# A transformer layer with a grouped mixture of experts on one core: the steps between the first norm and the first expert are rewritten

## The chip, the core and the metric

One Trainium2 chip (trn2); the program runs on one of its cores. The metric is device microseconds (us) of one execution. A core has five engines with queues of their own: PE (TensorE; its weight loads are shown as PEld), DVE (VectorE), ACT (ScalarE), POOL (GpSimd) and SP (SyncE, which here issues nearly all DMA). Each engine takes its instructions in program order and waits for the others by semaphores.

## What is computed

256 tokens (two blocks of 128) of width 2048 go through one layer: a projection, sparse attention and an mLSTM, gates, an output projection, a layer norm, then routed experts and a gated product ("PLE"), and a second layer norm. The part around the change:

```
h = layer_norm(DN_ALPHA * h + mix @ w_out, ln1_g, ln1_b)
grp_prob = softmax(h @ w_grp + b_grp)                      # 4 groups, the best one is taken
exp_logits = (h @ w_exp + b_exp)                           # 4 experts in each group
in_grp = the 4 logits of the chosen group; e_prob = softmax(in_grp)
e_p, e_idx = top_k(e_prob, 2); e_p = e_p / sum(e_p)        # two experts of the group
h = silu(h @ w_gate[e]) * (h @ w_up[e]) * combine; ff = h @ w_down[e]
ple = (p @ w_ple) * sigmoid(h @ w_ple_gate)
out = layer_norm(DN_ALPHA * h + ff + ple, ln2_g, ln2_b)
```

## The kernel before

**Stages.** Up to 916 us the kernel is a row of dense products. Each weight tile is split into a high and a low half by ACT (L1233) and DVE (L1720), and PE multiplies three times (L574, L575, L579). The last tile gives `RES`, the rows before the first norm. From 946.9 us on PE works through the experts in pairs of experts: `up(n)` has eight slots of 16 matmul records (L1017, gate and up weights), `down(n)` has four (L1069), and between them stand the chunks of the PLE gate (L928) and the scatters back to the rows.

**The ring.** Expert and gate weights come through a ring of 8 slots of 1 MB (`moe_ring`). SP issues 207 loads, always in the same order (L445). Loads 0 to 7 go out before 918 us. Load m from the eighth on waits until `ring_used` has reached m-7, that is, until PE is done with the slot that it overwrites. PE raises `ring_used` by 2 behind each slot of `up` and `down`.

**Between norm and experts** (916 to 947 us) the order on each queue is written out by hand:

- PE: `ple_product(0..3)` (L859), the turns of the normed rows to columns `row_turn(0..7)` (L875, four transposes each, banks 4, 5, 0, 1 in turn), `router()` (L885, 16 products of the router's weights with the turned columns, bank 4), `router_turn()` (L892), `ple_product(4..6)`, `expert_counts()` (L909 to L913, five products that count how many tokens each expert has), `ple_product(7)`, a quarter of the early gate product (L928, first of its four column parts), `row_table(4)` (L965), then `first_pairs(0)` and `first_pairs(1)` (L981, the gather of the tokens of the first group: the product of `selg` with the rows' high and low halves), then `up(0)`. The other three parts of the early gate product stand behind slot 6 of `up(0)`.
- DVE: the norm (L2149), the odd column turns (L2134), then the routing: `router_logits`, `best` once per token block (L2180 the eight largest, L2181 a copy, L2182 their replacement), `group_one_hot`, `expert_logits`, `best` twice again, `experts_one_hot` (L2206, raises `r_took`), `distances`, `slots` (L2239 to L2242), `select(0)` (L2252, eight comparisons that make `selg`), `h1_low(0..3)` (L2160, the low halves of the rows by quarters), `combine`, `overflow`. Most of these are tied by `link`, which makes DVE wait for its own last result.
- ACT: `pp_copy(0..3)` (L1502, PSUM to SBUF behind each PLE product), the even column turns (L1516), `high(0)` (L1507, the high half of block 0's rows, 128x2048), `pp_copy(4)`, `pp_copy(5)`, `high(1)` (block 1), `pp_copy(6)`, `pp_copy(7)`, then two exponentials (L1620, L1622, which want another function table, ACT_TABLE_LOAD), `row_table` (L1548), and `gained(0..7)` (L1568, which turns a gathered pair into `xg`, the input of `up(0)`).

`first_pairs` is held by these waits; a pair with i of 2 or more waits until ACT has emptied the bank of pair i-2, and slot 0 of `up(0)` wants `g_act` at 2:

```
if q == 0:
    pe.wait_ge(pp_c, 8)
pe.wait_ge(h1_lo, q + 1)
for i in (2 * q, 2 * q + 1):
    if i >= 2:
        pe.wait_ge(g_act, i - 1)
    gather_pair(i, B[6 + i % 2]).then_inc(g_mm, 1)
```

Of the kernel before, what the change touches and what calls it, by code (L numbers as in the profile page):

```python
# [137 lines left out]
def build(nc, x, p, w_in, kv_norm, w_ukv, m_i_bias, m_f_bias, w_proj_a, w_proj_m, w_out, ln1_g, ln1_b,  # L138
          w_grp, b_grp, w_exp, b_exp, w_gate, w_up, w_down, w_ple, w_ple_gate, ln2_g, ln2_b, out):
    with ExitStack() as ctx:  # L140
# [120 lines left out]
        tk8, r1, r2, r3, r4 = tiny(8), tiny(32), tiny(32), tiny(32), tiny(16)  # L261
        mg, me, gd, ed = tiny(16), tiny(16), tiny(8), tiny(8)
        oneh, combw, gp, top2 = tiny(8), tiny(8), tiny(4), tiny(8)
        took, cum, tot, tslot = tiny(2 * NE), tiny(2 * NE), tiny(NE), tiny(2 * NE)
# [233 lines left out]
        def _(pl):  # L498
# [58 lines left out]
            g.iota(iota[:], pattern=[[1, CAP]], base=0, channel_multiplier=0,  # L557
# [7 lines left out]
        def _(pe):  # L565
# [312 lines left out]
            def router():  # L878

                pe.wait_ge(r_in, 32)  # L880
                pe.wait_ge(hT_act, 4)
                pe.wait_ge(hT_dve, 4)
                for k in range(KT):
                    j = 32 * (k % 4)
                    last = mm(B[4][j:j + 32, 0:TOK], wr[:, k, :], hT[:, k, :], start=k < 4, stop=k >= KT - 4)  # L885
                last.then_inc(r_part, 1)
# [11 lines left out]
            for i in range(8):  # L898
                row_turn(i)
            router()  # L900
            router_turn()
            for n in range(4, 7):
                ple_product(n)

            def expert_counts():
# [5 lines left out]
                mm(c[:, NE:2 * NE], upper[:], two, start=False, stop=True)  # L911
                mm(c[:, 2 * NE:3 * NE], ones[:], one, start=True, stop=False)
                mm(c[:, 2 * NE:3 * NE], ones[:], two, start=False, stop=True).then_inc(r_cum, 1)  # L913
# [107 lines left out]
            def up(n):  # L1021
# [7 lines left out]
                for i in range(UP_SLOTS):  # L1029
# [9 lines left out]
                    if n == 0 and i == 6:  # L1039
                        ple_rows(EW[:, 0, :], 2, 0, True, True, (1, 2, 3)).then_inc(early_used, 1)  # L1040
# [75 lines left out]
            ple_product(7)  # L1116
            pe.wait_ge(bank_free[1], 20)
            pe.wait_ge(early_in[0], 16)
            ple_rows(EW[:, 0, :], 2, 0, True, True, (0,))
            pe.wait_ge(sel_ready, 1)  # L1120
            row_table(4, selT_mm)
            pe.wait_ge(h1_hi, NT)
# [94 lines left out]
        def _(ac):  # L1217
# [286 lines left out]
            def high(a):  # L1504

                ac.wait_ge(z_ready, NT)
                fn(h1h[:, a, :, :].rearrange("p t q -> p q t"), RES[:, a, :].rearrange("p (q t) -> p q t", t=KT),  # L1507
                   ACT.Copy).then_inc(h1_hi, 1)
# [11 lines left out]
            pp_copy(4)  # L1520
            pp_copy(5)
            high(1)
            pp_copy(6)
            pp_copy(7)
            def used(kind, n, i):

                ac.wait_ge(ring_used, LOAD_AT[kind, n, i, 1] + 1)
# [178 lines left out]
        def _(dv):  # L1706
# [448 lines left out]
            def h1_low(q):  # L2155

                dv.wait_ge(h1_hi, NT)
# [358 lines left out]
```

## Time and profile before

| | |
|---|---|
| median of 3 runs | 1491.25 us (1491.24 to 1491.49) |
| the profiled execution | 1491.56 us |
| its span, first to last instruction | 1489.8 us |
| PE busy | 1462.4 us (98% of the span) |
| DVE, ACT, POOL busy | 706.8, 513.1, 57.3 us |
| DMA, over the whole span | 405.92 MB, mean 272 GB/s |
| granted TensorE clock, mean | 0.998 |

Times in the profile are us from the first instruction. A row of the timeline gives start, duration, engine, line, operation, what it writes and reads, and the form; consecutive instructions of one line on one engine are merged (x8), and the bracket tells how long the engine sat idle before it and what ended that.
### The profile page before, as it was taken

To read this page: it belongs to the slowest core of one execution; us is meant where nothing else is said; L and a number is where in the kernel's file an instruction comes from. 1 tells how busy PE (TensorE), PEld (TensorE's weight loads), DVE (VectorE), ACT (ScalarE), POOL (GpSimd) and SP (SyncE) were. 2 spreads that over 40 slices of the span, in tenths; PEclk is the share of its full clock that TensorE was granted. 3 is DMA by queue.
4 is the path that set the end of the run, shared out by engine and by line. 5 is a ranking of instruction groups with operands and counts; after the bars stand their busy time and mean duration, and the time that the engine had idled before them with its cause. 6 is when DMAs were issued, how large, how long until landed. Compare 5 with 4: busy or idle time off the path is not lost.

```text
span 1489.8 us, 16743 instructions
## 1 busy us (share of the span) xinstructions
PE 1462.4 (98%) x6572; PEld 997.4 (67%) x6572; DVE 706.8 (47%) x974; ACT 513.1 (34%) x690; POOL 57.3 (4%) x63
## 2 busy tenths in 40 slices
PE   9999999999999999999999999999999998999998
PEld 7887788888778888888888887534434443454443
DVE  5546675467656665454555555431221231143336
ACT  4444444455545454444444434411000100031111
POOL 0000000053300000000000000000000000000000
PEclk9999999999999999999999999999999999999999
DMA  8654586754454585655567977599999999999995
GB/s 311 201 169 162 167 238 197 226 197 142 142 195 142 184 241 193 199 187 190 190 209 229 349 238 244 209 419 421 416 411 419 394 388 420 417 393 415 415 407 212
DMA packets 138287, 405.92 MB, mean 272 GB/s; under 512 B 14296, under 2 KB 18016, under 8 KB 113248
## 3 DMA queue, kind: packets, MB, share of 16 engines
q1 hardware_dynamic: 129472, 396.52, 73.0%
q10 hardware_dynamic: 8736, 8.33, 1.7%
q8 instruction: 51, 0.84, 0.2%
q14 instruction: 28, 0.23, 0.0%
HBM read 392.76 MB, written 4.20 MB: 266 GB/s over the span
## 4 chain that ended last, share of the span: by engine, by line
PE 92%; DMA 5%; DVE 1%; ACT 0%; issue 0%; POOL 0%; SPq 0%; POOLq 0%; DVEq 0%; ACTq 0%
PE bank L574 19%; PE bank L575 19%; PE bank L579 19%; PE bank L1017 12%; PE bank L1069 5%; PE bank L928 5%; DMA moe_ring<-in_w_gate_dram 3%; DMA moe_ring<-in_w_down_dram 2%; PE bank L981 2%; PE bank L1112 1%; PE bank L1097 1%; PE bank L1113 1%; PE bank L733 1%; PE bank L755 1%; PE bank L950 1%; PE bank L951 1%
## 5 line engine op out<-in xcount | busy, mean ns | idle before, releaser
L1720 DVE TENSOR_TENSOR w_lo<-w_ring,w_hi 128x1024 fp32r<-128x1024 f32 (+1 forms) x312 | 381.4, 1225 | 286.1 <-ACT w_hi L1233 285.0
L1233 ACT ACTIVATE w_hi<-w_ring 128x1024 fp32r<-128x1024 f32 (+1 forms) x312 | 327.3, 1051 | 329.8 <-PE bank L579 329.8
L574 PE MATMUL bank<-w_hi,xT_hi 128*128 128x512 f32 (+1 forms) x864 | 344.3, 399 | 1.7 <-ACT w_hi L1233 1.7
L575 PE MATMUL bank<-w_hi,xT_lo 128*128 128x512 f32 (+1 forms) x864 | 334.6, 387 | 0.0
L1017 PE MATMUL bank<-moe_ring,xg 128*64 128x512 f32 x1024 | 226.1, 594 | 10.4 <-DMA moe_ring<-in_w_gate_dram 6.7
L579 PE MATMUL bank<-w_lo,xT_hi 128*128 128x512 f32 (+1 forms) x864 | 229.1, 387 | 0.0
L574 PEld LDWEIGHTS bank<-w_hi,xT_hi 128*128 128x128 f32 x864 | 162.3, 188 | 38.5 <-issue 4.6
L575 PEld LDWEIGHTS bank<-w_hi,xT_lo 128*128 128x128 f32 x864 | 162.4, 188 | 32.8 <-issue 1.9
L579 PEld LDWEIGHTS bank<-w_lo,xT_hi 128*128 128x128 f32 x864 | 161.5, 188 | 32.9
L1017 PEld LDWEIGHTS bank<-moe_ring,xg 128*64 128x64 f32 x1024 | 72.9, 137 | 156.7 <-issue 156.1
L1069 PE MATMUL bank<-moe_ring,moe_hiddenT 128*64 128x512 f32 x448 | 100.2, 595 | 1.8 <-DMA moe_ring<-in_w_down_dram 1.8
L2323 DVE TENSOR_TENSOR res<-res,bank 128x512 f32<-128x512 f32 x62 | 38.4, 681 | 105.3 <-issue 80.4
L1069 PEld LDWEIGHTS bank<-moe_ring,moe_hiddenT 128*64 128x64 f32 x448 | 31.6, 137 | 61.7 <-issue 60.4
L928 PE MATMUL bank<-moe_ring,h1T 128*128 128x512 f32 x144 | 63.4, 593 | 0.0
L2286 DVE TENSOR_TENSOR ple_sig<-bank,ple_sig 128x512 f32<-128x512 f32 x24 | 15.5, 686 | 73.8 <-PE bank L928 57.1
L574 PE MATMUL bank<-w_hi,mixT_hi 128*128 128x512 f32 x128 | 50.1, 391 | 0.0
L575 PE MATMUL bank<-w_hi,mixT_lo 128*128 128x512 f32 x128 | 49.8, 389 | 0.0
L574 PE MATMUL bank<-w_hi,ymT_hi 128*128 128x512 f32 x128 | 49.8, 389 | 0.0
L574 PE MATMUL bank<-w_hi,yaT_hi 128*128 128x512 f32 x128 | 49.8, 389 | 0.0
L575 PE MATMUL bank<-w_hi,yaT_lo 128*128 128x512 f32 x128 | 49.8, 389 | 0.0
L575 PE MATMUL bank<-w_hi,ymT_lo 128*128 128x512 f32 x128 | 49.8, 389 | 0.0
L928 PEld LDWEIGHTS bank<-moe_ring,h1T 128*128 128x128 f32 x144 | 27.2, 190 | 31.6 <-issue 31.0
(292 smaller groups left out, 1352.0 us busy)
## 6 DMA issues: line engine op xcount, KB each, us to landing
w_ring<-in_w_in_dram SPq DMA_DIRECT2D x103, 1024.0 KB, 5.0
moe_ring<-in_w_gate_dram SPq DMA_DIRECT2D x64, 1024.0 KB, 9.7
moe_ring<-in_w_up_dram SPq DMA_DIRECT2D x64, 1024.0 KB, 10.5
moe_ring<-in_w_down_dram SPq DMA_DIRECT2D x64, 1024.0 KB, 11.1
w_ring<-in_w_proj_a_dram SPq DMA_DIRECT2D x16, 1024.0 KB, 5.1
w_ring<-in_w_proj_m_dram SPq DMA_DIRECT2D x16, 1024.0 KB, 5.1
w_ring<-in_w_out_dram SPq DMA_DIRECT2D x16, 1024.0 KB, 5.2
moe_ring<-in_w_ple_gate_dram SPq DMA_DIRECT2D x15, 1024.0 KB, 13.2
```

Of the source, the lines that this page charges most:

```text
L574: mm(b, lh(k, m), WH[:, s, kk, 0:width], start=start and kk == 0, stop=False)
L575: mm(b, ll(k, m), WH[:, s, kk, 0:width], start=False, stop=False)
L579: last = mm(b, lh(k, m), WL[:, s, kk, 0:width], start=False, stop=stop and kk == 1)
L733: last = mm(B[4 + j][:, r * w:r * w + w], aqT[:, 4 * (u % 4) + 2 * j + r, a * P:a * P + P], kT[:, 0:w], start=True, stop=True)
L928: ins = mm(B[b + a][:, :], hT[:, k, a * P:a * P + P], w[:, t * NC:t * NC + NC], start=first and t == 0, stop=last and t == 3)
L981: last = mm(b[:, kk * TOK:kk * TOK + TOK], src[:, a, 2 * i + kk, :], selg[:, a, :], start=part == 0 and a == 0, stop=part == 1 and a == 1)
L1017: last = mm(B[b0 + i % 2][CAP * e:CAP * e + CAP, :], xg[:, k, (e0 + e) * CAP:(e0 + e) * CAP + CAP], w[e][:, t * NC:t * NC + NC], start=k = ...
L1069: last = mm(B[4 + c][CAP * e:CAP * e + CAP, :], src[:, k, CAP * e:CAP * e + CAP], w[e][:, c * NC:c * NC + NC], start=k == 0, stop=k == 3)
L1233: fn(WH[:, h % 4, :, 0:width], W32[:, h // 2, 2 * (h % 2):2 * (h % 2) + 2, 0:width], ACT.Copy).then_inc(hi_ready, 1)
L1720: v.tensor_tensor(WL[:, h % 4, :, 0:width], W32[:, h // 2, 2 * (h % 2):2 * (h % 2) + 2, 0:width], WH[:, h % 4, :, 0:width].bitcast(F32), A ...
L2286: last = v.tensor_tensor(psg[:, a, :], B[b + a][:, :], psg[:, a, :], ALU.add)
L2323: v.tensor_tensor(r, r, B[b0 + a][:, :], ALU.add).then_inc(y_add, 1)
```

## The change

Five edits, all between the first norm and the end of `up(0)`:

1. The router's 16 products go out in four steps of four, step 0 after `row_turn(5)`, the rest after `row_turn(7)`; they write bank 2 in place of bank 4.
2. The routing on DVE handles both token blocks in one call of `best`; three copies go; `slots` is one instruction in place of four (the count's table starts at 1 in place of 0, and the totals are copied later, in `combine`); `expert_counts` raises `r_cum` after three of its five products.
3. `select` makes `selg` in two comparisons of 128x256 in place of eight of 128x64.
4. `high` goes by quarters of the columns for both blocks (two instructions of 128x512 each), placed between the `pp_copy` calls; the last comes after `pp_copy(7)`. `h1_low(q)` waits for quarter q alone.
5. On PE: two in place of three PLE products before `expert_counts`, `ple_product(6)` after it, then `row_table(4)`, then `ple_product(7)`. The first part of the early gate product moves behind slot 6 of `up(0)`, to the other three.

```diff
-            g.iota(iota[:], pattern=[[1, CAP]], base=0, channel_multiplier=0,
+            g.iota(iota[:], pattern=[[1, CAP]], base=1, channel_multiplier=0,
...
-            def router():
-                pe.wait_ge(r_in, 32)
-                pe.wait_ge(hT_act, 4)
-                pe.wait_ge(hT_dve, 4)
-                for k in range(KT):
+            def router(step):
+                if step == 0:
+                    pe.wait_ge(r_in, 32)
+                    pe.wait_ge(bank_free[1], 20)
+                pe.wait_ge(hT_act, step + 1)
+                pe.wait_ge(hT_dve, step + 1)
+                for k in range(4 * step, 4 * step + 4):
                     j = 32 * (k % 4)
-                    last = mm(B[4][j:j + 32, 0:TOK], wr[:, k, :], hT[:, k, :], start=k < 4, stop=k >= KT - 4)
-                last.then_inc(r_part, 1)
+                    last = mm(B[2][j:j + 32, 0:TOK], wr[:, k, :], hT[:, k, :], start=step == 0, stop=step == 3)
+                if step == 3:
+                    last.then_inc(r_part, 1)
...
-            for i in range(8):
+            for i in range(6):
                 row_turn(i)
-            router()
+            router(0)
+            row_turn(6)
+            row_turn(7)
+            for step in range(1, 4):
+                router(step)
             router_turn()
-            for n in range(4, 7):
-                ple_product(n)
+            ple_product(4)
+            ple_product(5)
...
                 mm(c[:, NE:2 * NE], ones[:], one, start=True, stop=False)
-                mm(c[:, NE:2 * NE], upper[:], two, start=False, stop=True)
-                mm(c[:, 2 * NE:3 * NE], ones[:], one, start=True, stop=False)
-                mm(c[:, 2 * NE:3 * NE], ones[:], two, start=False, stop=True).then_inc(r_cum, 1)
+                mm(c[:, NE:2 * NE], upper[:], two, start=False, stop=True).then_inc(r_cum, 1)
+                mm(B[3][:, 0:NE], ones[:], one, start=True, stop=False)
+                mm(B[3][:, 0:NE], ones[:], two, start=False, stop=True).then_inc(r_cum, 1)
...
                     if n == 0 and i == 6:
-                        ple_rows(EW[:, 0, :], 2, 0, True, True, (1, 2, 3)).then_inc(early_used, 1)
+                        pe.wait_ge(early_in[0], 16)
+                        ple_rows(EW[:, 0, :], 2, 0, True, True).then_inc(early_used, 1)
...
             expert_counts()
-            ple_product(7)
-            pe.wait_ge(bank_free[1], 20)
-            pe.wait_ge(early_in[0], 16)
-            ple_rows(EW[:, 0, :], 2, 0, True, True, (0,))
+            ple_product(6)
             pe.wait_ge(sel_ready, 1)
             row_table(4, selT_mm)
-            pe.wait_ge(h1_hi, NT)
+            ple_product(7)
             first_pairs(0)
             first_pairs(1)
...
-            def high(a):
+            def high(q):
                 ac.wait_ge(z_ready, NT)
-                fn(h1h[:, a, :, :].rearrange("p t q -> p q t"), RES[:, a, :].rearrange("p (q t) -> p q t", t=KT),
-                   ACT.Copy).then_inc(h1_hi, 1)
+                for a in range(NT):
+                    last = fn(h1h[:, a, 4 * q:4 * q + 4, :].rearrange("p t q -> p q t"),
+                              RES[:, a, :].rearrange("p (q t) -> p q t", t=KT)[:, :, 4 * q:4 * q + 4], ACT.Copy)
+                last.then_inc(h1_hi, 1)
...
             high(0)
             pp_copy(4)
+            high(1)
             pp_copy(5)
-            high(1)
+            high(2)
             pp_copy(6)
             pp_copy(7)
+            high(3)
...
-                dv.wait_ge(h1_hi, NT)
+                dv.wait_ge(h1_hi, q + 1)
...
-                v.tensor_copy(rrow[:], B[4][:, 0:TOK]).then_inc(r_row, 1)
+                v.tensor_copy(rrow[:], B[2][:, 0:TOK]).then_inc(r_row, 1)
...
+                v.tensor_tensor(two(rp)[:, :, 0:4], two(B[5][:, 0:40])[:, :, 0:4], brt[:, 0:4].unsqueeze(1).to_broadcast([P, 2, 4]),
+                                ALU.add)
                 link(v.tensor_tensor(two(lgt), two(B[5][:, 0:40]), brt.unsqueeze(1).to_broadcast([P, 2, 20]), ALU.add))
-                link(v.tensor_copy(two(rp)[:, :, 0:4], two(lgt)[:, :, 0:4]))
-            def best(a, n, found, out):
-                link(v.max(found[:, 8 * a:8 * a + 8], rp[:, 16 * a:16 * a + 16]))
-                link(v.tensor_copy(tk8[:, 0:n], found[:, 8 * a:8 * a + n]))
-                link(v.match_replace(out[:, 16 * a:16 * a + 16], tk8, rp[:, 16 * a:16 * a + 16], TAKEN))
+            def best(n, found, out):
+                for a in range(NT):
+                    last = v.max(found[:, 8 * a:8 * a + 8], rp[:, 16 * a:16 * a + 16])
+                link(last)
+                link(v.tensor_copy(two(tk8)[:, :, 0:n], two(found)[:, :, 0:n]))
+                for a in range(NT):
+                    last = v.match_replace(out[:, 16 * a:16 * a + 16], tk8[:, 8 * a:8 * a + 8], rp[:, 16 * a:16 * a + 16], TAKEN)
+                link(last)
...
-                    last = v.tensor_reduce(r4[:, 8 + 4 * a:12 + 4 * a],
+                    last = v.tensor_reduce(rp[:, 16 * a:16 * a + 4],
                                            r3[:, NE * a:NE * a + NE].rearrange("p (g e) -> p e g", g=GROUPS), AX, ALU.add)
                 link(last)
-                link(v.tensor_copy(two(rp)[:, :, 0:4], two(r4[:, 8:16])))
...
             def combine():
+                dv.wait_ge(r_cum, 2)
+                link(v.tensor_copy(tot, B[3][:, 0:NE]))
...
-                link(v.tensor_copy(cum, B[5][:, P:P + 2 * NE]))
-                link(v.tensor_copy(tot, B[5][:, P + 2 * NE:P + 3 * NE]))
-                link(v.tensor_tensor(cum, cum, took, ALU.mult))
-                link(v.tensor_scalar(tslot, cum, -1.0, None, ALU.add))
+                link(v.tensor_tensor(tslot, B[5][:, P:P + 2 * NE], took, ALU.mult))
...
                 for a in range(NT):
-                    for e in range(EPG):
-                        t = NE * a + EPG * g + e
-                        last = v.tensor_scalar(selg[:, a, CAP * e:CAP * e + CAP], iota[:], tslot[:, t:t + 1], None,
-                                               ALU.is_equal)
+                    t = NE * a + EPG * g
+                    last = v.tensor_tensor(selg[:, a, :].rearrange("p (e c) -> p e c", e=EPG),
+                                           iota[:, :].unsqueeze(1).to_broadcast([P, EPG, CAP]),
+                                           tslot[:, t:t + EPG].unsqueeze(2).to_broadcast([P, EPG, CAP]), ALU.is_equal)
```

## Rows read from the trace of the kernel before

**Rows 1.** Windows of the expert stage: us, busy times, clock, DMA share, GB/s
```profile
954.00:958.00 4.00, 4.00 (x30) 3.22 (x32) 0.00 (x0) 2.30 (x6) 0.00 (x0) 1.00 1.01 426
962.00:963.00 1.00, 1.00 (x8) 0.36 (x6) 0.00 (x0) 0.00 (x0) 0.00 (x0) 1.00 0.73 205
950.56:1447.80 497.24, 483.09 (x2154) 212.54 (x2151) 124.48 (x188) 70.81 (x116) 0.00 (x0) 1.00 1.00 409
```
**Rows 2.** Timeline of SP's queue, the ring's loads around 950 and 980 us
```profile
950.56 0.81 SPq L445 DMA_DIRECT2D moe_ring<-in_w_gate_dram  x2
...
960.57 0.80 SPq L445 DMA_DIRECT2D moe_ring<-in_w_gate_dram  x2
...
976.56 0.81 SPq L445 DMA_DIRECT2D moe_ring<-in_w_gate_dram  x2
985.49 0.80 SPq L445 DMA_DIRECT2D moe_ring<-in_w_up_dram  x2
```
**Rows 3.** Timeline, turned columns and router products
```profile
923.50 3.97 PE L875 MATMUL bank<-ident,res 128*128 128x128 f32 x32 [0.29 <-DVE res L2149]
924.78 3.72 DVE L2134 TENSOR_SCALAR h1T<-bank,small 128x256 f32<-128x256 f32 x8 [1.34 <-PE bank L875]
928.65 1.93 PE L885 MATMUL bank<-h1T,w_router 128*32 128x256 f32 x32 [1.18 <-DVE h1T L2134]
930.64 0.42 DVE L2171 COPY router_rows<-bank 128x256 f32<-128x256 f32 x1 [2.14 <-PE bank L885]
```
**Rows 4.** Timeline of DVE, the routing steps
```profile
932.29 0.18 DVE L2180 MAX8 small<-small 128x8 f32<-128x16 f32 x1
...
932.77 0.16 DVE L2182 MATCH_REPLACE8 small<-small 128x16 f32<-128x16 f32 x1
...
936.23 0.26 DVE L2206 TENSOR_TENSOR small<-small 128x16 f32<-128x16 f32 x2
```
**Rows 5.** Timeline of PE, from the counts to the first expert
```profile
936.82 0.29 PE L909 MATMUL bank<-small,upper 128*128 128x16 f32 x2
...
937.85 1.96 PE L859 MATMUL bank<-wple,pT 128*128 128x512 f32 x4
...
939.65 1.88 PE L928 MATMUL bank<-ple_early,h1T 128*128 128x512 f32 x4
...
940.97 0.96 PE L965 MATMUL bank<-ident_r,moe_sel 128*128 128x128 f32 x4
...
944.79 0.47 PE L981 MATMUL bank<-moe_sel,h_hi 128*128 128x256 f32 x2 [0.25 <-ACT xg L1568]
...
946.86 7.09 PE L1017 MATMUL bank<-moe_ring,xg 128*64 128x512 f32 x32
```
**Rows 6.** Timeline of ACT, from the last product copies to the gathered pairs
```profile
939.34 1.12 ACT L1502 ACTIVATE ple_products<-bank 128x512 f32<-128x512 f32 x2
940.47 1.28 ACT L1620 ACT_TABLE_LOAD   x1
...
941.98 0.59 ACT L1548 ACTIVATE moe_selT<-bank 128x512 fp32r<-128x512 f32 x1
...
943.63 1.97 ACT L1568 ACTIVATE xg<-bank,small 128x256 f32<-128x256 f32 x4 [1.07 <-PE bank L981]
```
**Rows 7.** Groups by form: count, busy us, mean ns of one, idle before
```profile
L1507 ACT ACTIVATE h_hi<-res 128x2048 fp32r<-128x2048 f32 x2 | 7.6, 3780 | 0.0
...
L1629 ACT ACTIVATE ln_g<-ln_g 128x2048 f32<-128x2048 f32 x1 | 1.9, 1907 | 0.0
...
L2160 DVE TENSOR_TENSOR h_lo<-res,h_hi 128x512 fp32r<-128x512 f32 x8 | 8.0, 1083 | 0.0
```
**Rows 8.** PE's first transposes, its last matmuls, and the window behind them
```profile
1.59 4.53 PE L625 MATMUL bank<-ident 128*128 128x128 f32 x20 [1.59 <-POOL ident L508]
...
1477.66 5.31 PE L1169 MATMUL bank<-res,rstd_diagonal 128*128 128x512 f32 x12
...
1482.00:1486.00 4.00, 0.98 (x3) 0.15 (x1) 0.31 (x1) 1.19 (x2) 0.00 (x0) 0.90 0.76 275
```

More of the change, by code:

```diff
@@ L260, in build @@
         brt, lgt, rp = tiny(20), tiny(40), tiny(32)
-        tk8, r1, r2, r3, r4 = tiny(8), tiny(32), tiny(32), tiny(32), tiny(16)
+        tk8, r1, r2, r3, r4 = tiny(16), tiny(32), tiny(32), tiny(32), tiny(16)
         mg, me, gd, ed = tiny(16), tiny(16), tiny(8), tiny(8)
         oneh, combw, gp, top2 = tiny(8), tiny(8), tiny(4), tiny(8)
-        took, cum, tot, tslot = tiny(2 * NE), tiny(2 * NE), tiny(NE), tiny(2 * NE)
+        took, tot, tslot = tiny(2 * NE), tiny(NE), tiny(2 * NE)
         cg, flagf, tslg = tiny(4), tiny(1), tiny(2 * EPG)
@@ L2217, in distances @@
                 for a in range(NT):
-                    last = v.tensor_scalar(ed[:, 4 * a:4 * a + 4], r4[:, 8 + 4 * a:12 + 4 * a], me[:, 8 * a:8 * a + 1], None,
+                    last = v.tensor_scalar(ed[:, 4 * a:4 * a + 4], rp[:, 16 * a:16 * a + 4], me[:, 8 * a:8 * a + 1], None,
                                            ALU.subtract)
@@ L2347, in _ @@
             router_logits()
-            best(0, 1, mg, r3)
-            best(1, 1, mg, r3)
+            best(1, mg, r3)
             group_one_hot()
             expert_logits()
-            best(0, 2, me, r1)
-            best(1, 2, me, r1)
+            best(2, me, r1)
             experts_one_hot()
```

## The prediction

> **What bounds the kernel now.** I read the windows first. From 950.56 us, when PE has used up the first ring slot, to 1447.80 the DMA engines are busy at a share of 1.00 and move 409 GB/s, while the granted clock is 1.00 and PE is busy for 483 of 497 us [rows 1]. The reader is to see that weights are delivered at the rate the engines have, from the first refill on. The queue of SP shows what starts this stream: two loads at 950.56, each pair behind one slot of `up(0)` [rows 2]. So the change can do two things alone: move the start of the stream, and make holes in it. All behind the start shifts with it; what an engine saves beside it is worth nothing.
>
> Then the timeline between norm and first expert. Two chains meet there. DVE turns columns, PE forms the router's products, DVE routes until 936.23 + 0.26 = 936.49 and then selects, and PE's `row_table` at 940.97 is the first to read the selection [rows 3 to 5]. PE fills its waits with other products. What ends last is ACT and PE in turn: the first gathered pair is emptied by ACT from 943.63, PE waits for that until 944.79, and `up(0)` starts at 946.86 [rows 5, 6]. ACT could have begun at 942.47 (its `row_table` copy starts at 941.98, the next one 0.49 later), so it had 1.16 us of slack.
>
> **Part 1, router in step.** Before, 32 transposes took 3.97 us, the last column was turned at 924.78 + 3.72 = 928.50, and 32 records of router products took 1.93 [rows 3]. Four products now stand ahead of turns 6 and 7: a quarter of 1.93, some 0.45, and 0.1 for the changes between kinds. DVE then ends its columns at 929.05. Only the last four products are behind that: 0.15 to start, 0.63 for issue and drain. The copy of the rows starts at 929.9 in place of 930.64: 0.75 sooner.
>
> **Part 2, routing.** One call of `best` goes from 932.29 to 932.93, 0.67 with the link, and there are four [rows 4]. Two blocks in one call add an overlapped maximum (0.10) and a replacement (0.17): 0.95 in place of 1.35, twice, 0.80 saved. A copy of some 0.2 between linked steps goes, another becomes an overlapped instruction (0.1). With the 0.75 `r_took` comes 1.85 sooner, at 934.64.
>
> **Part 3, PE's order.** `ple_product(5)` is issued by 934.4, so the counts start at 934.7. Before, they started at 936.82 and product 7 1.03 later, at 937.85 [rows 5]. Now product 6 starts at 935.75. But between counts and product 7 stand product 6 (1.80 issued) and `row_table` (0.80 less the overlap of 0.4): product 7 starts at 937.97, 0.1 later than before, although routing is 1.85 ahead. `slots` (three instructions fewer) and the two comparisons are ready by 936.7, bounded by twice the 1.08 us that a 128x512 with such strides takes [rows 7]: at 937.8 at the latest, about when `row_table` wants them, so they cost nothing. DVE's gain of over 3 us ends here, in a wait for PE.
>
> **Part 4, ACT.** This is the step that decides. Two product copies took 1.12, so the second started at 939.86, 2.0 behind product 7's start [rows 5, 6]; now 939.98. Before, the function table followed at once. Now `high(3)` stands between. Its price: the 128x2048 took 3.78 where a contiguous one took 1.91 [rows 7]. A contiguous copy of 512 took 0.60 (two in 1.12, overlapped by 0.1 [rows 6]), so the fixed part is 0.17, and an element here costs 1.76 ns: 1.07 for 512 elements and 0.97 from start to start. DVE's instructions of exactly the quarter's shape took 1.08. Two of them put 1.94 into the chain. The chain behind it is unchanged: table load 1.28, two small exponentials, `row_table`, then the gathered pairs. ACT can begin them at 942.47 + 0.12 + 1.94 = 944.53, in place of 943.63: **0.90 later**. `high(0..2)` hide in ACT's waits for products (it waits for product 6 until 937.75 and for product 7 until 939.98). PE's first two pairs start when copy 7 is done, at 940.6, 1.8 sooner than before, and then PE waits for ACT. `up(0)` starts at 946.86 + 0.90 = 947.76.
>
> The Trainium skill (ScalarE: Activation LUTs, "What ACT_TABLE_LOAD costs") adds a drain of about 1.38 us to each load of 1.28. Here the load starts 0.01 us behind a copy's end [rows 6], so the trace has no such drain; an estimate by the page would put the result 1.4 us later, and I go by the row.
>
> **Part 5, the early gate product.** Before, its first part took 1.72 of PE ahead of the gather [rows 5]. Taken from there it gains nothing, since ACT ends later. Behind slot 6 it delays slot 7's release, 985.49 before [rows 2], by 1.72. Is the stream covered? Fourteen loads were issued from 950.56 up to the pair at 976.56. A load's data begin some 2.3 us behind its issue: the hole at 962 to 963, share 0.73 [rows 1], ends 2.4 behind the issue of the fifth and sixth load at 960.57 [rows 2]. Fourteen loads of 1.049 MB at 426 GB/s are 34.5 us; with the hole of some 0.5 and the start at 952.9 they end at 987.9. The next one, issued at 985.49, begins at 987.8. There was next to no cover. Of 1.72 all could pass into the stream, or less if the queue holds more than this sum shows; bounds 0 and 1.7, nearer the upper, I take **1.3**. PE itself arrives later too, but waits for weights before and after, so nothing more is added.
>
> **Part 6, PE's new idle time.** From 942.9 (end of pairs 0 and 1) to 945.7, PE does nothing: 2.8 us, and 0.8 before pair 0. Through PE's waits in the expert stage, 497.24 - 483.09 = 14.2 us together, the granted clock stays at 1.00 [rows 1], but behind the last matmul, which ends at 1477.66 + 5.31 = 1482.97, the window 1482 to 1486 has a mean of 0.90 [rows 8]: 0.8 us of 4 at 0.50, a fall 2.2 us after PE stopped. 2.8 is longer. At the lower level 20 transposes took 4.53 (0.21 apart), at the upper 32 took 3.97 (0.11 apart) [rows 3, 8]: from 1.59 to some 7.2 us work ran at half pace before the clock rose, 5.6 us, which cost 2.8. Bounds for a fall here are 0 and 2.8; between them, since PE has just been busy, I take 1.4.
>
> The skill (TensorE: Matmul & The Clock Gate, "What's actually happening") has the same two levels and lets an idle engine fall to the lower one.
>
> **Sum.** 0.9 + 1.3 + 1.4 = 3.6 us later. Against the profiled execution (span 1489.8, 1.8 around it, 1491.56) that is 1495.1; the median of the runs is 0.3 lower, 1491.25, so 1494.8.
>
> **The rivals.**
>
> *The clock holds.* The same without the 1.4: 1493.4. For it: PE's waits in the expert stage changed nothing [rows 1], and the fall after 2.2 us is a single case, at the end [rows 8].
>
> *The quarters cost by the run, not by the element.* The high halves are read in runs of 16 and now of 4. If the excess of 1.87 us of a 128x2048 belongs to its 128 runs, a quarter's instruction takes 2.5 us. ACT is then full: a pair of 4.8 in place of 1.94 puts the gathered pairs at about 951.5, the sum at +9, 1500. It decides from 2.8 us a pair on, where ACT no longer waits for product 7; below that each 0.1 counts once. Against it: DVE's instructions in runs of 4 cost about as much an element (2.1 ns) as ACT's in runs of 16 (1.85) [rows 7].
>
> *The gather decides by the selection.* If `high(3)` is much cheaper (contiguous pace, 1.0 a pair) or the chain behind it holds nothing, `up(0)` starts when PE can: two pairs from 940.6, then at the earliest 945.0, 1.8 sooner. With the move covered by queued loads that is 1489.4; with both steps saving more than I count, 1488. For it: DVE is over 3 us ahead. Against it: ACT's order is fixed, and the table load stood right behind the last copy.
>
> *The change does less than it says*: steps that overlap less in DVE. 0.5 us more on routing moves product 7 and all behind it by 0.5, inside the range.
>
> **How the numbers follow.** A measurement tells about 0.2% from no change, 3.0 us, so 1488.3 to 1494.2 is "the same". My forecast with the fallen clock gets 0.45, nearly all of it slower. The held clock gets 0.35, nearly all the same. The costly quarters get 0.07, slower. The gather by selection gets 0.13, half of it over the bound. Together: faster 0.07, same 0.43, slower 0.50. The range for 8 in 10 goes from the held clock with half the cost of part 5 (1492) less some of the third rival, 1491.4, to the forecast with the full 1.7 and 2.8: 1496.6. The forecast's own range is 1493.4 to 1496.6.
>
> **What would show each step.** Right: in the changed trace DVE's `r_took` near 934.6 and its comparisons done by 937; product 7 near 938; ACT's table load near 942.5 behind two L1507-like instructions of about 1.07; ACT at the gathered pairs from 944.5; the first refill by SP near 951.5; a hole in DMA between 986 and 991; a granted clock of 0.50 for some us from 944 on. Wrong: quarters of 2.5 us, a table load ahead of `high(3)`, PE in `up(0)` before 946.9, or a DMA share of 1.00 through 986 to 991 with the end less than 1 us behind.

## The result, and the profile after

The changed kernel takes 1498.0 us (median of 9 runs, 1493.98 to 1498.67) against 1491.49 (9 runs, 1490.48 to 1494.35): ratio 1.0035, 95% interval 1.0026 to 1.0045. A second measurement (`e9_changed_again`) gives 1.0031, 1.0018 to 1.0044. By these ratios it is 4.6 to 5.2 us slower; the medians lie further apart in the first measurement (6.5) and less in the second (1496.27 against 1492.27, 4.0). The sum said 3.6 later, a time of 1494.8. 1498.0 lies above the stated range, whose upper end is 1496.6; the second measurement's median lies just inside it. All the runs told of here are fast ones, but for one disturbed run of e3 (3849 us), which its ratio leaves out.

The profiled execution takes 1498.67 us, its span is 1496.9. PE was busy for 4.5 us more than before, with as many records of work in it:

```profile
span 1496.9 us, 16724 instructions
PE 1466.9 (98%) x6572; PEld 998.8 (67%) x6572; DVE 703.3 (47%) x945; ACT 513.7 (34%) x696; POOL 57.1 (4%) x63
```

The timeline of the changed kernel between norm and first expert, the three engines together (answers to [rows 3 to 6]; its norm ended 0.57 us later, 924.07 for 923.50, so that much comes off every later time):

```profile
924.07 3.06 PE L875 MATMUL bank<-ident,res 128*128 128x128 f32 x24 [0.29 <-DVE res L2158]
927.06 0.64 PE L887 MATMUL bank<-h1T,w_router 128*32 128x256 f32 x8
927.63 1.17 PE L875 MATMUL bank<-ident,res 128*128 128x128 f32 x8
...
930.67 0.42 DVE L2180 COPY router_rows<-bank 128x256 f32<-128x256 f32 x1 [0.84 <-PE bank L887]
...
935.02 0.26 DVE L2219 TENSOR_TENSOR small<-small 128x16 f32<-128x16 f32 x2
935.34 0.40 PE L916 MATMUL bank<-small,upper 128*128 128x16 f32 x2
...
936.44 0.76 DVE L2263 TENSOR_TENSOR moe_sel<-iota,small 128x256 fp32r<-128x256 f32 x2
...
938.67 1.93 PE L859 MATMUL bank<-wple,pT 128*128 128x512 f32 x4
...
940.64 0.60 ACT L1507 ACTIVATE ple_products<-bank 128x512 f32<-128x512 f32 x1 [1.56 <-PE bank L859]
941.13 2.07 ACT L1513 ACTIVATE h_hi<-res 128x512 fp32r<-128x512 f32 x2
943.22 1.28 ACT L1629 ACT_TABLE_LOAD   x1
...
945.21 1.93 ACT L1577 ACTIVATE xg<-bank,small 128x256 f32<-128x256 f32 x4
946.36 0.77 PE L988 MATMUL bank<-moe_sel,h_hi 128*128 128x256 f32 x2 [2.90 <-ACT xg L1577]
...
949.79 0.65 PE L1024 MATMUL bank<-moe_ring,xg 128*64 128x512 f32 x2
```

DVE's comparisons are done by 937.20. Everything after that waits: `row_table` for PE, the copy of product 7 for PE, `high(3)` and the table load one behind the other on ACT, and PE 2.90 us for ACT. The windows then show three things, in this order: PE works at the lower clock for 3.4 us, the DMA engines have too little to do once near 991 (a share of 0.67 over 2 us; below, "the hole"), and the clock falls a second time in `up(3)`:

```profile
942.00:946.00 4.00, 1.47 (x13) 1.26 (x11) 3.68 (x9) 3.97 (x8) 0.00 (x0) 1.00 0.00 0
946.00:949.40 3.40, 3.04 (x14) 3.07 (x15) 1.17 (x8) 2.08 (x5) 0.00 (x0) 0.50 0.00 0
990.00:992.00 2.00, 2.00 (x12) 0.65 (x10) 1.69 (x4) 0.00 (x0) 0.00 (x0) 1.00 0.67 147
1120.00:1123.50 3.50, 1.18 (x6) 0.57 (x8) 0.00 (x0) 0.00 (x0) 0.00 (x0) 1.00 1.03 392
1123.50:1127.00 3.50, 3.50 (x10) 1.20 (x8) 0.00 (x0) 0.00 (x0) 0.00 (x0) 0.51 1.01 420
```

The slot of `up(3)` in which this second fall lies takes 5.35 us, where the same 16 records take 3.65 in the kernel before; PE waited 2.34 us for weights ahead of it (PE's timeline):

```profile
1122.32 5.35 PE L1024 MATMUL bank<-moe_ring,xg 128*64 128x512 f32 x16 [2.34 <-DMA moe_ring<-in_w_gate_dram]
```

The mean granted clock of the other eight runs is a rough sign of how many falls they had. Of all nine runs, six have 0.996 or 0.997 (the profiled one, with two falls, has 0.997) and took 1496.99 to 1498.67 us; two have 0.998 and took 1493.98 and 1495.52; one has 0.999 and took 1498.11 all the same.

SP's queue, changed kernel (answers to [rows 2]). The first refill is 2.92 later than before, the release behind slot 6 is 4.65 later, the last load of PLE gate weights 6.83:

```profile
953.48 0.81 SPq L445 DMA_DIRECT2D moe_ring<-in_w_gate_dram  x2
...
990.14 0.80 SPq L445 DMA_DIRECT2D moe_ring<-in_w_up_dram  x2
...
1128.07 0.43 SPq L445 DMA_DIRECT2D moe_ring<-in_w_ple_gate_dram  x1
...
1429.43 0.38 SPq L445 DMA_DIRECT2D moe_ring<-in_w_ple_gate_dram  x1
```

The same two loads in the kernel before:

```profile
1121.88 0.43 SPq L445 DMA_DIRECT2D moe_ring<-in_w_ple_gate_dram  x1
...
1422.60 0.38 SPq L445 DMA_DIRECT2D moe_ring<-in_w_ple_gate_dram  x1
```

### One table for all kernels

SP issues the same loads in the same order in every kernel here, so its rows cut the span into like stretches. I took, from each kernel's profile: **A**, from the first column turn (L875, 923.50 before) to the first refill (950.56); **B**, from there to the fourth load of PLE gate weights (1106.52 before); **C**, from there to the fifth (1121.88), which holds PE's longest waits for weights; **D**, from there to the last of them (1422.60), where no edit reaches. "Gate part" says where the first part of the early gate product stands.

| kernel | gate part | A | B | C | D |
|---|---|---|---|---|---|
| before | ahead of the gather | 27.06 | 155.96 | 15.36 | 300.72 |
| changed | slot 6 | 29.41 | 157.54 | 17.05 | 301.36 |
| changed, again (e9) | slot 6 | 29.57 | 157.53 | 15.39 | 300.90 |
| e1 | slot 6 | 27.05 | 157.36 | 17.22 | 300.23 |
| e2 | slot 6 | 28.06 | 159.57 | 16.99 | 301.45 |
| e3 | slot 6 | 26.09 | 157.53 | 17.09 | 300.25 |
| e4 | in the gap | 28.06 | 155.85 | 15.54 | 301.38 |
| e5 | slot 6 | 25.41 | 157.49 | 17.22 | 301.29 |
| e6 | ahead of the gather | 26.17 | 155.94 | 14.68 | 301.71 |
| e7 | ahead of the gather | 27.76 | 155.93 | 14.41 | 299.95 |
| e8 | slot 6 | 27.05 | 157.43 | 15.91 | 300.28 |
| e10 | slot 6 | 28.05 | 157.33 | 15.82 | 299.92 |
| e11 | ahead of the gather | 25.87 | 155.83 | 14.49 | 300.29 |
| e12 | ahead of the gather | 25.56 | 155.99 | 15.39 | 301.89 |

A is the work between norm and first expert, B shows a hole in the stream, C a second fall of the clock: 16.99 to 17.22 with it. Without it C still varies, from 14.41 to 15.91. D is the measure's own noise: 299.95 to 301.89 for a stretch that is the same in all. A single profile's end says nothing about 1 us; A and B do, and C does for a fall. Each row is one execution, and not always a typical one: e2's is the slowest of its 12 runs (1499.32, median 1494.05), the changed kernel's the slowest of 9, e11's nearly the fastest of its 11.

### The profile page after: what moved, and what is told of

It is laid out like the page before. It is cut to its first block, busy times and chain, and to the rows that moved or that the text cites. A ratio compares the mean times of both kernels' runs of the same rounds, so it can differ in the third digit from the quotient of the medians.

```text
span 1496.9 us, 16724 instructions
## 1 busy us (share of the span) xinstructions
PE 1466.9 (98%) x6572; PEld 998.8 (67%) x6572; DVE 703.3 (47%) x945; ACT 513.7 (34%) x696; POOL 57.1 (4%) x63
## 4 chain that ended last, share of the span: by engine, by line
PE 91%; DMA 6%; DVE 1%; ACT 1%; SPq 1%; issue 0%; POOL 0%; POOLq 0%; DVEq 0%; ACTq 0%
PE bank L574 19%; PE bank L579 18%; PE bank L575 18%; PE bank L1024 12%; PE bank L1077 5%; PE bank L935 5%; DMA moe_ring<-in_w_gate_dram 3%; DMA moe_ring<-in_w_down_dram 2%; PE bank L988 2%; PE bank L1120 1%; PE bank L1105 1%; PE bank L1121 1%; PE bank L733 1%; PE bank L755 1%; PE bank L957 1%; SPq L364 1%
```

## The experiments

Each ran in turn with the kernel before on the same chip, and its ratio is to that kernel's runs there (medians 1491.67 for e1 to e4, 1491.78 for e5 to e8, 1492.27 for e9 to e12; three chips). Where a ratio and a difference of medians do not agree, both are given.

### e1: only the gate part moved

Kernel before, with part 5's move alone.

```diff
-                        ple_rows(EW[:, 0, :], 2, 0, True, True, (1, 2, 3)).then_inc(early_used, 1)
+                        pe.wait_ge(bank_free[1], 20)
+                        pe.wait_ge(early_in[0], 16)
+                        ple_rows(EW[:, 0, :], 2, 0, True, True).then_inc(early_used, 1)
...
-            pe.wait_ge(bank_free[1], 20)
-            pe.wait_ge(early_in[0], 16)
-            ple_rows(EW[:, 0, :], 2, 0, True, True, (0,))
```

> The kernel before with one edit: the first part of the early gate product moves from ahead of the gather to behind slot 6 of up(0). Theory (the ring's stream has no cover there): the start of up(0) stays where it is, within 0.2 us; slot 7's release comes 1.7 us later than its neighbours; a hole of over half a microsecond shows in the DMA windows some 36 to 41 us behind the first refill; the end is 1.0 to 1.7 us later than before. Rival (queued loads cover it): no hole, the end within 0.5 us of before. Rival (the stage behind is what the time hangs on): later by over 3 us, with a low granted clock somewhere in the expert stage.

Measured: 1494.74 us, ratio 1.0019 (1.0009 to 1.0030), 2.8 us. Three views of its profile, first SP's queue, whose release went from 985.49 to 987.28:

```profile
987.28 0.80 SPq L445 DMA_DIRECT2D moe_ring<-in_w_up_dram  x2
```

then windows, one at the hole and one behind PE's longest wait:

```profile
987.00:989.00 2.00, 2.00 (x12) 0.71 (x10) 1.97 (x8) 0.00 (x0) 0.00 (x0) 1.00 0.61 156
1119.50:1123.00 3.50, 3.50 (x10) 1.30 (x12) 0.00 (x0) 0.00 (x0) 0.00 (x0) 0.51 1.05 425
```

then PE's timeline in `up(3)`:

```profile
1119.46 3.54 PE L1017 MATMUL bank<-moe_ring,xg 128*64 128x512 f32 x7 [2.22 <-DMA moe_ring<-in_w_gate_dram]
```

The hole is where the forecast had it. In the table A is untouched (27.05), B is 1.4 longer, and C another 1.9: PE waits for weights for 2.22 in place of 1.54, the clock falls there, and the slot behind the wait takes 5.35 us in place of 3.65. So the end is later than the 1.0 to 1.7 us expected, and the low clock that the last rival named is there beside the hole. The kernel before waits at the same place, for less, and the clock holds:

```profile
1117.82 3.65 PE L1017 MATMUL bank<-moe_ring,xg 128*64 128x512 f32 x16 [1.54 <-DMA moe_ring<-in_w_gate_dram]
```

### e2: the gap before the second pair filled

The changed kernel with three products between the two gathers, which nobody reads.

```diff
             first_pairs(0)
+            for _ in range(3):
+                mm(B[0][:, :], ident[:], pT[:].rearrange("p k n -> p (k n)"), start=True, stop=True)
             first_pairs(1)
```

> The changed kernel with three products of 128x512 whose result nobody reads, put between the first and the second two gather pairs, where PE waits 2.9 us for ACT. Theory (the clock fell because PE stood still): no low clock at that place, up(0) starts 1.4 us sooner than in the changed kernel, and the median is 1.4 us lower, near 1496.6, or some 3 to 4 lower if the second fall of the clock in the expert stage is a consequence of the first. Rival (the clock falls on its own account, whatever PE does there): the same low stretch, the time unchanged or later by the products that are added.

Measured: 1494.05 us, ratio 1.0016 (1.0007 to 1.0025). PE's timeline, then windows around it and in `up(3)`:

```profile
942.87 2.74 PE L1130 MATMUL bank<-pT,ident 128*128 128x512 f32 x6
...
945.92 0.47 PE L988 MATMUL bank<-moe_sel,h_hi 128*128 128x256 f32 x2 [0.31 <-ACT xg L1579]
```

```profile
944.00:948.00 4.00, 3.69 (x21) 2.36 (x20) 2.63 (x13) 3.53 (x10) 0.00 (x0) 1.00 0.00 0
1120.20:1123.60 3.40, 3.40 (x10) 1.21 (x8) 0.00 (x0) 0.00 (x0) 0.00 (x0) 0.52 1.06 415
```

More work on PE, and A falls from 29.41 and 29.57 to 28.06: the clock's fall there costs 1.4 to 1.5 us. The second fall stays, so it is no consequence of the first. The expectation for that case was some 5 us over the kernel before; it is 2.4, less than the first fall alone accounts for, and that isn't explained.

### e3: `high(3)` off ACT's chain

```diff
             pp_copy(7)
-            high(3)
...
             for i in range(8):
+                if i == 2:
+                    high(3)
```

(the second place is ACT's loop of `gained(0..7)`)

> The changed kernel with high(3) behind the second emptied pair, out of ACT's chain to the first pair. Theory (ACT's chain sets the start of up(0), and the clock fell as its consequence): ACT reaches the pairs 1.9 us sooner, no low clock there, up(0) starts 3.3 us sooner than in the changed kernel, near 946.5; the median near 1494.7, with what is left over due to the hole that the moved gate part makes. Rival (product 7 and the selection hold the gather, ACT has slack): up(0) less than 1 us sooner, the time as before within 1 us of 1498.

Measured: 1491.99 us, ratio 1.0000 (0.9990 to 1.0010). ACT's and PE's timelines:

```profile
940.10 1.28 ACT L1628 ACT_TABLE_LOAD   x1
...
943.25 0.47 PE L988 MATMUL bank<-moe_sel,h_hi 128*128 128x256 f32 x2 [0.94 <-ACT xg L1576]
...
945.33 1.08 PE L1024 MATMUL bank<-moe_ring,xg 128*64 128x512 f32 x4
```

A is 26.09: 1.0 sooner than before and 3.4 sooner than with the change. B and C show the hole and the second fall unchanged. By the table that sums to 1.57 + 1.73 - 0.97 = 2.3 us later; the expectation was some 3 us later; the runs show none of it, with 1.5 us to each side. The profile shows one execution, and whether the others had the second fall too isn't known.

### e4: the gate part inside the gap

The changed kernel with that part between `first_pairs(0)` and `first_pairs(1)`, where e2 had its filling; the totals move to bank 1, since bank 3 is its own, and PE's wait for `combined` goes ahead of slot 1 of `up(0)` (so too in e6, e11 and e12).

```diff
             first_pairs(0)
+            pe.wait_ge(early_in[0], 16)
+            ple_rows(EW[:, 0, :], 2, 0, True, True, (0,))
             first_pairs(1)
...
-                mm(B[3][:, 0:NE], ones[:], one, start=True, stop=False)
-                mm(B[3][:, 0:NE], ones[:], two, start=False, stop=True).then_inc(r_cum, 1)
+                mm(B[1][:, 0:NE], ones[:], one, start=True, stop=False)
+                mm(B[1][:, 0:NE], ones[:], two, start=False, stop=True).then_inc(r_cum, 1)
```

> The changed kernel with the first part of the early gate product put into the gap between the first and second two gather pairs (the totals of the counts go to bank 1). Theory: it fills 1.7 of the 2.9 us, so the clock holds (-1.4), and slot 6 of up(0) is as long as before, so the hole goes (-1.5): the median near 1495.0, up(0) near 948.4. Rival (the expert stage's own rhythm costs the rest): the start of up(0) is 1.4 us sooner and the end is not, over 1497.

Measured: 1493.12 us, ratio 1.0003 (0.9985 to 1.0022). Its windows where the hole had been:

```profile
988.00:990.00 2.00, 2.00 (x12) 0.69 (x10) 0.00 (x0) 0.00 (x0) 0.00 (x0) 1.00 0.97 406
```

No hole (B 155.85), no fall, A as in e2 (28.06). One edit takes away both. The medians are 1.45 us apart, the ratio says 0.4; the table's sum is 1.1, and the expectation was 3.5.

### e5: exponentials ahead of the last product copy

e3, and the two exponentials with their table load stand ahead of `pp_copy(7)`.

```diff
             pp_copy(6)
+            ac.wait_ge(r_one, 1)
+            fn(r2[:, 0:8], gd, ACT.Exp).then_inc(r_exp, 1)
+            ac.wait_ge(r_log, 1)
+            fn(r2[:, 8:16], ed, ACT.Exp).then_inc(r_exp, 1)
             pp_copy(7)
```

> The changed kernel with high(3) behind the second emptied pair, and the two exponentials with their table load ahead of the last product copy, where ACT waits for PE. The gate part stays moved. Theory: ACT reaches the first pair when PE has gathered it; up(0) starts 0.5 to 0.8 us sooner than in e3; the hole and the fall of the clock near 1119 us stay, since they hang on the moved gate part: the median 0.6 below e3's, 1491.4 or a little less. Rival (the front no longer counts): as e3, within 0.2.

Measured: 1491.53 us, ratio 0.9999 (0.9990 to 1.0008). ACT's timeline:

```profile
936.98 0.60 ACT L1507 ACTIVATE ple_products<-bank 128x512 f32<-128x512 f32 x1
937.60 1.28 ACT L1533 ACT_TABLE_LOAD   x1
...
941.06 1.98 ACT L1580 ACTIVATE xg<-bank,small 128x256 f32<-128x256 f32 x4 [0.82 <-PE bank L988]
```

The load hides in ACT's wait for PE, and A is 25.41, the shortest of all; the hole and the second fall are still there. As in e3 the table's sum, 1.53 + 1.86 - 1.65 = 1.7, is above the ratio's interval. So two kernels with the hole show none of its cost in their times; why isn't known.

### e6: e5 with the gate part ahead of the gather again

e5, the totals in bank 1, and in PE's order:

```diff
             ple_product(7)
+            pe.wait_ge(early_in[0], 16)
+            ple_rows(EW[:, 0, :], 2, 0, True, True, (0,))
             first_pairs(0)
```

(`combine` also goes ahead of the last `h1_low`, so that its result is there for slot 1)

> As e5, and the first part of the early gate product stands ahead of the gather again (the totals of the counts in bank 1, DVE's combine ahead of the last h1_low). Theory (a short front, no hole, no fall of the clock): up(0) starts 0.8 us sooner than in the kernel before, no low clock near 1119, the median 0.8 below before's, 1490.7 where before has 1491.5. Rival (the expert stage gives it back, by longer waits for weights): no difference from before, within 0.2 us.

Measured: 1490.74 us, ratio 0.9995 (0.9985 to 1.0004). A is 26.17, B and C are free of hole and fall. The medians are 1.0 us apart, near the 0.8 expected, but the interval takes in no change: no difference from before is shown.

### e7: only the high halves in quarters

The kernel before with edit 4 alone.

```diff
-            def high(a):
+            def high(q):
...
-            pp_copy(5)
             high(1)
+            pp_copy(5)
+            high(2)
             pp_copy(6)
             pp_copy(7)
+            high(3)
```

> The kernel before with edit 4 alone: high halves in quarters, high(3) behind pp_copy(7). Theory (high(3) delays ACT's table load and the pairs behind it): ACT comes to the first pair 0.9 us later than before, up(0) starts 0.9 later, PE waits some 1.2 us and the clock holds, the end is 0.9 later. Rival (the quarters pay, since the first low halves need not wait for all high halves): the first pair sooner than 943.6 and the end not later.

Measured: 1491.99 us, ratio 1.0007 (0.9996 to 1.0018). ACT's timeline, then PE's:

```profile
939.98 1.98 ACT L1507 ACTIVATE h_hi<-res 128x512 fp32r<-128x512 f32 x2
941.98 1.28 ACT L1623 ACT_TABLE_LOAD   x1
...
943.96 1.93 ACT L1571 ACTIVATE xg<-bank,small 128x256 f32<-128x256 f32 x4
...
945.12 0.47 PE L981 MATMUL bank<-moe_sel,h_hi 128*128 128x256 f32 x2 [0.96 <-ACT xg L1571]
```

A is 0.70 longer: the quarter takes from ACT's chain what the forecast said, less 0.2. PE's wait is 0.96 here, not 2.90, and the clock holds. The times don't tell 0.7 from nothing.

### e8: e1 with the wait in `up(3)` filled

Two products nobody reads, where PE would wait for slot 2's weights.

```diff
+                    if n == 3 and i == 2:
+                        pe.wait_ge(e_hid, 3)
+                        for _ in range(2):
+                            mm(B[1][:, :], ident[:], wr[:].rearrange("p k n -> p (k n)"), start=True, stop=True)
```

> The kernel of e1 (before, gate part moved) with two products of 128x512 that nobody reads, put ahead of slot 2 of up(3), where PE waits 2.2 us for weights in e1. Theory (that wait is long enough for the clock to fall, and the slow matmuls behind it release the ring late): no low clock near 1119 us, the end 1.5 to 2 us sooner than e1, near 1493. Rival (the fall costs nothing, since PE waits for weights anyway): the low clock gone and the time as in e1, 1494.7, within 0.5.

Measured: 1493.07 us, ratio 1.0012 (1.0003 to 1.0021). Windows of the place:

```profile
1118.00:1124.00 6.00, 6.00 (x27) 2.35 (x27) 0.00 (x1) 0.53 (x1) 0.00 (x0) 1.00 1.04 417
```

The clock holds, C goes from 17.22 to 15.91, B stays at 157.43. Against their bases e8 is 1.8 us below e1 by the medians and 1.0 by the ratios, but the two intervals (1.6 and 1.3 us to each side) overlap, so the times alone don't show it; the table says 1.3. The hole and the second fall are two costs, and the fall is not needed for the hole. That the filling holds the clock rests on two profiles, this one and e10's; e9's shows that it can also hold without.

### e9: the changed kernel again

> The changed kernel itself, for a second profile and an interval of its own beside the runs of this call. Theory (ACT's wait lowers the clock near 946 us, the wait for weights near 1122 us lowers it again): both low stretches again or, where a profile lacks one of them, an end that is 1.4 us or more sooner; ratio to before 1.003 to 1.004. Rival (the falls of the first profile were chance): no low stretch, ratio about 1.0015.

Measured: 1496.27 us, ratio 1.0031 (1.0018 to 1.0044). The first fall is there, the second isn't (two windows), though PE waits as long as in e1, one slot earlier (PE's timeline):

```profile
945.70:949.10 3.40, 3.40 (x16) 3.40 (x16) 0.87 (x6) 1.77 (x4) 0.00 (x0) 0.50 0.00 0
...
1120.00:1124.00 4.00, 2.66 (x14) 0.91 (x12) 0.00 (x0) 0.00 (x0) 0.00 (x0) 1.00 1.06 410
```

```profile
1116.84 3.65 PE L1024 MATMUL bank<-moe_ring,xg 128*64 128x512 f32 x16 [2.21 <-DMA moe_ring<-in_w_up_dram]
```

### e10: both waits filled

e2 and e8's filling in the changed kernel.

```diff
+                    if n == 3 and i == 2:
+                        pe.wait_ge(e_hid, 3)
+                        for _ in range(2):
+                            mm(B[1][:, :], ident[:], wr[:].rearrange("p k n -> p (k n)"), start=True, stop=True)
...
+            for _ in range(3):
+                mm(B[0][:, :], ident[:], pT[:].rearrange("p k n -> p (k n)"), start=True, stop=True)
```

> The changed kernel with both waits filled by products that nobody reads: three between the gather pairs (as e2), two ahead of slot 2 of up(3) (as e8). Theory (what is left is high(3)'s 0.9 and the hole's 1.5, less what the front gains): no low clock inside the span, the median 2 us over before and 4 to 5 under the changed kernel. Rival (the two falls do not add): no better than e2, 2.4 over before, with its low stretch near 1120 gone all the same.

Measured: 1493.77 us, ratio 1.0013 (1.0003 to 1.0024). A 28.05, B 157.33, C 15.82: without the clock, the change costs the quarter (1.0) and the hole (1.4). The median is 2.5 us under e9's, so five products that do nothing seem to make it faster, though the two intervals just overlap. That is less than the 4 to 5 expected; e9's profile has only one of the two falls.

### e11: router, routing and selection alone

The changed kernel with parts 4 and 5 undone (long `high`, PE's old order).

```diff
             expert_counts()
-            ple_product(6)
+            ple_product(7)
+            pe.wait_ge(early_in[0], 16)
+            ple_rows(EW[:, 0, :], 2, 0, True, True, (0,))
             pe.wait_ge(sel_ready, 1)
             row_table(4, selT_mm)
-            ple_product(7)
+            pe.wait_ge(h1_hi, NT)
```

> Edits 1 to 3 alone (router in step, routing for both blocks, two comparisons), with ACT's and PE's order as before. Theory (the chain through PE and ACT sets the start, DVE's part is covered): DVE's selection is ready 1.5 to 2 us sooner, up(0) starts 0.3 to 0.6 us sooner, the median at most 0.6 lower. Rival (the selection is what the first expert waits for): up(0) over 1.5 us sooner, and the end with it.

Measured: 1491.33 us, ratio 0.9994 (0.9985 to 1.0003). DVE's and ACT's timelines:

```profile
936.79 0.76 DVE L2262 TENSOR_TENSOR moe_sel<-iota,small 128x256 fp32r<-128x256 f32 x2
...
939.44 1.28 ACT L1628 ACT_TABLE_LOAD   x1
```

A is 25.87, 1.2 sooner than before, where 0.3 to 0.6 was expected; the time itself isn't shown to differ. The first three edits do what they are for; the other two gave it back and put 2.4 more on A, 1.4 to 1.5 of it by the clock.

### e12: e6 with product 4 ahead of the router's turn

PE's order: product 4, `router_turn`, products 5 and 6, counts, product 7, gate part, `row_table`, pairs.

```diff
+            ple_product(4)
             router_turn()
-            ple_product(4)
             ple_product(5)
+            ple_product(6)
...
-            ple_product(6)
-            pe.wait_ge(sel_ready, 1)
-            row_table(4, selT_mm)
             ple_product(7)
             pe.wait_ge(early_in[0], 16)
             ple_rows(EW[:, 0, :], 2, 0, True, True, (0,))
+            pe.wait_ge(sel_ready, 1)
+            row_table(4, selT_mm)
```

> As e6, with ple_product(4) ahead of router_turn, where PE waits 0.5 us for DVE's copy, three products ahead of the counts, and row_table behind the gate part. Theory (in e6 PE is the bound between router and up(0), every wait of PE that is filled counts once): up(0) up to 0.5 us sooner than in e6, 1.3 to 1.5 sooner than before; the median 0.5 under e6's, 1 to 1.5 under before's. Rival (routing, now 1.2 us later, becomes the bound): row_table and the gather wait for the selection, up(0) as in e6 or later.

Measured: 1490.87 us, ratio 0.9988 (0.9979 to 0.9997), against 1492.27: 1.4 us (by the ratio 1.8) faster than the kernel before, the only variant whose interval lies wholly on that side. PE's waits between 925 and 960 are gone but for two:

```profile
PE bank L989 <- ACT xg L1582: 0.2, 1, 0.2
PE bank L887 <- DVE h1T L2146: 0.2, 1, 0.2
```

In `up(3)` it has a wait of 2.30, longer than e1's although there is no hole ahead of it (B is 155.99), and the clock holds; PE's timeline and the window around it:

```profile
1116.56 3.65 PE L1025 MATMUL bank<-moe_ring,xg 128*64 128x512 f32 x16 [2.30 <-DMA moe_ring<-in_w_gate_dram]
```

```profile
1112.00:1120.00 8.00, 5.70 (x28) 1.87 (x24) 0.00 (x0) 0.00 (x0) 0.00 (x0) 1.00 1.03 411
```

## Why the prediction was right, and where it was wrong

**What bounds the kernel** held. In every kernel B falls into one of two lengths, by the gate part's place, whatever A is (e2 apart), and the front shows only as A.

**Parts 1 to 3** held within 0.2 us once the later norm is taken off. The rows' copy stood at 930.67 - 0.57 = 930.10 (forecast 929.9), `r_took` at 935.28 - 0.57 = 934.71 (934.64), product 7 at 938.10 (937.97). DVE was ahead by over 3 us for nothing in the changed kernel, as said. What e11 adds: with the old order behind it, the routing does carry 1.2 us to the first refill. Some 0.5 of that is PE's own row of work, which starts sooner behind the router (product 7 at 936.82 + 0.49 = 937.31, for 937.85). Another 0.5 is a wait of the kernel before that the prediction doesn't have, PE's for DVE's low halves, ahead of the gather:

```profile
942.40 0.48 PE L981 MATMUL bank<-moe_sel,h_hi 128*128 128x256 f32 x2 [0.47 <-DVE h_lo L2160]
```

So DVE's part was on the path there, not only ACT's and PE's.

**Part 4** held. The pair of quarters took 2.07 (forecast 1.94), and ACT reached the gathered pairs at 945.21 - 0.57 = 944.64 (forecast 944.53; e9, whose norm ended 0.10 sooner than before: 944.53 + 0.10 = 944.63). e7 shows it alone: 0.7 more in A for 0.9. e2, e4 and e10, with the clock held, have 1.0. The row also decided rightly on the table load: it starts 0.02 us behind the copy, so no drain of 1.38, as the Trainium skill adds one (ScalarE: Activation LUTs, "What ACT_TABLE_LOAD costs"), was seen here or in e3, e5, e7 or e11.

**Part 6, the fall near 946,** came as forecast: after an idle time of 2.90, 3.4 us at 0.50. It cost 1.4 to 1.5 (A of e2 and e10 against the changed kernel; forecast 1.4). The size is partly luck: 1.4 was the middle between bounds of 0 and 2.8. The forecast's `up(0)` was 947.76 + 1.4 = 949.2; it stood at 949.22 with the norm taken off, and at 949.37 in e9, taken alike. The rival in which the clock holds is refuted, and so are the costly quarters and the gather that waits only for the selection. e4 shows besides that fall and hole come from one decision, where the gate part stands.

**Part 5 is where it failed**, in its last sentence: "PE itself arrives later too, but waits for weights before and after, so nothing more is added." The hole itself was well sized: B is 1.4 to 1.6 longer in all kernels with the part at slot 6, except e2 (3.6), for 1.3 forecast, a value picked between 0 and 1.7.

But the waits that were to absorb PE's lateness did not stay as they were. With the part at slot 6 and the wait left open (the changed kernel, e9, e1, e2, e3, e5) the longest one in `up(3)` was 2.1 to 2.9 us; with the part elsewhere it was 1.3 to 1.7, except 2.30 in e12. That the later stream lengthens it is thus what most profiles suggest, and not shown. In five of those six the clock fell behind it, and C was 17.0 to 17.2, where it is 15.4 to 15.9 with the clock held (e8, e9, e10). That puts 1.4 us on a term that the prediction had at nothing. The time lost there is not won back: with the fall the fifth load of PE gate weights goes out later by as much, and D is no shorter.

In its size the term of part 5 is 1.5 + 1.4 in place of 1.3 where the second fall occurs, and 1.5 where it doesn't (e9). With it the sum is 1.0 + 1.4 + 1.5 = 3.9 without the second fall and 5.3 with it; the ratios say 4.6 and 5.2. The prediction had looked for a fall of the clock in the one gap that it had seen open, and took the waits of the stage, in which "the granted clock stays at 1.00", as safe at any length.

Not settled: the times of e3 and e5, some 2 us under their table sums, and e2's B, 2 us above the others. The latter comes from the slowest of e2's 12 runs, with the granted clock at 1.00 through B, so it may be that run's and not the kernel's.

## What to carry to other kernels

Work taken out of a stretch that waits for another engine is not free to move: it may be what keeps TensorE's clock up (e2, e4 and e10 put work there, and the clock held), and where it lands it may hold back the release that a saturated stream lives on (e1). When a change makes a stream later, read again every wait behind it, with the granted clock beside it, not only the place that was edited. And judge an edit of 1 to 3 us by stretches between like instructions of the profile: a stretch that was the same in all kernels moved by 2 us for no reason that was found.

## What was not expected of the hardware

**The clock falls inside a stage that is otherwise busy.** PE's waits of 2.14 to 2.90 us were followed by 3.4 us at 0.50 in the changed kernel (twice), e1, e2, e3, e5 and e9, and each fall cost 1.2 to 1.7 us by A or C. But waits of 2.21 (e9) and 2.30 (e12) left it at 1.00, so the length of the wait alone doesn't decide. What does was not found.

**Identical work varies.** Stretch D took from 299.95 to 301.89 us in 14 profiles, with the granted clock at 1.00 through it in all of them. Nor does the clock explain all the scatter of whole runs: one run of the changed kernel took 1498.11 at a mean clock of 0.999, as much as others at 0.996. What the rest is was not tried.
